# TensorE's order alone, between the input products and the stream of expert rows, redone in a one-layer hybrid encoder step

## What is computed

```python
z = rmsnorm(x) @ w_in                 # q | k | v | g | a | b, 512 columns each
o = retention(rotary(q), rotary(k), v)            # 4 heads of 128, causal with decay, state per head
y_ret  = silu(g) * groupnorm(o)
u      = a * sigmoid(b)
y_conv = silu(layernorm(depthwise_conv31(u)))
x = x + concat(y_ret, y_conv) @ w_out
h = rmsnorm(x)
qry = h @ peer_query                  # 8 heads x 2 x 128
top16 of qry . keys per half, then top16 of the 256 sums -> 16 experts of 16384 per row and head
x = x + sum_e softmax_e * gelu(h . down[e]) * up[e]
out = rmsnorm(x)
```

## Time and profile before

| | |
|---|---|
| median of 3 runs | 1663.01 us (1662.77 to 1663.81) |
| the profiled execution's own time | 1664.46 us |
| its span | 1662.7 us |
| PE busy | 1383.8 us (83%) |
| DVE busy | 1174.9 us (71%) |
| ACT busy | 573.3 us (34%) |
| POOL busy | 716.7 us (43%) |
| gather queue | 570.46 MB, 82.9% of 16 DMA engines' span |
| HBM read | 604.19 MB |

### The profile page before, as it was taken

One profiled execution on the slowest core, in us unless ns is written; L12 is line 12 of the kernel. 1 busy time (PEld: TensorE's weight loads), 2 busy tenths in 40 slices (PEclk: granted clock), 3 DMA queues, 4 the chain that ended last, 5 costly groups with the idle time before them and its releaser, 6 DMA issues.

```text
span 1662.7 us, 14018 instructions
## 1 busy us (share of the span) xinstructions
PE 1383.8 (83%) x4311; PEld 678.6 (41%) x4311; DVE 1174.9 (71%) x2555; ACT 573.3 (34%) x1785; POOL 716.7 (43%) x633
## 2 busy tenths in 40 slices
PE   7999999998898789778977897789779877777733
PEld 6744465554353335324433443344324423332311
DVE  3997758966876777677767776777777777676755
ACT  3112231632433333333333333333433333333342
POOL 0004624644444445444444444445444444444552
PEclk9999999999899999999999999999999999999955
DMA  7203227999999999999999999999999999999996
GB/s 293 102 1 100 110 77 279 371 421 422 422 420 422 421 422 420 422 421 422 420 422 421 422 421 422 421 421 421 421 422 421 421 422 420 419 420 421 414 421 256
DMA packets 87978, 608.39 MB, mean 366 GB/s; under 512 B 11104, under 2 KB 13664, under 8 KB 16224
## 3 DMA queue, kind: packets, MB, share of 16 engines
q0 software_dynamic: 78336, 570.46, 82.9%
q1 hardware_dynamic: 9568, 37.04, 5.9%
HBM read 604.19 MB, written 2.88 MB: 365 GB/s over the span
## 4 chain that ended last, share of the span: by engine, by line
DMA 44%; PE 37%; DVE 10%; issue 3%; ACT 3%; POOL 2%; DVEq 0%; SPq 0%; POOLq 0%
DMA arena<-experts,expert 44%; PE ps L1686 18%; PE ps L1549 8%; PE ps L1649 5%; DVE arena L1329 4%; PE ps L1529 4%; POOL arena L603 2%; ACT weight L907 1%; ACT late L917 1%; PE ps L1508 1%; DVE cst L1305 0%; DVE cst L1308 0%; DVE picked L1312 0%; PE ps L1620 0%; ACT gl L899 0%
## 5 line engine op out<-in xcount | busy, mean ns | idle before, releaser
L1686 PE MATMUL ps<-arena,late 128*128 128x512 f32 x2016 | 950.3, 624 | 206.0 <-ACT late L917 205.7
L603 POOL DMA_INDIRECT arena<-experts,expert x544 | 645.2, 1186 | 732.4 <-PE ps L1686 627.5
L1329 DVE CUSTOM_DVE_ANT_0 arena<-arena,hn 128x1024 f32<-128x1024 f32 x544 | 656.7, 1222 | 384.9 <-DMA arena<-experts,expert 381.8
L1686 PEld LDWEIGHTS ps<-arena,late 128*128 128x128 f32 x2016 | 387.3, 198 | 745.0 <-issue 450.7
L899 ACT ACTIVATE gl<-dots 128x2 f32<-128x2 f32 (+1 forms) x274 | 55.8, 204 | 814.3 <-DVE dots L1329 814.3
L917 ACT ACTIVATE late<-cst,weight 128x128 f32<-128x128 f32 (+1 forms) x536 | 183.5, 389 | 8.8
L907 ACT ACTIVATE weight<-gl,gate 128x1 f32<-128x1 f32 x544 | 130.7, 287 | 8.9
L1549 PE MATMUL ps<-arena,hT 128*128 128x512 f32 x256 | 112.3, 598 | 0.0
L1649 PE MATMUL ps<-hT,region_b 128*128 128x272 f32 x448 | 106.9, 392 | 0.0
L1649 PEld LDWEIGHTS ps<-hT,region_b 128*128 128x128 f32 x448 | 85.1, 190 | 27.9 <-issue 12.4
L1072 DVE SCALAR_TENSOR_TENSOR region_b<-region_b,par 128x574 f32<-128x574 f32 x120 | 92.5, 813 | 4.5
(11 more groups left out here) (174 smaller groups left out, 872.1 us busy)
## 6 DMA issues: line engine op xcount, KB each, us to landing
arena<-weights SPq DMA_DIRECT2D x6, 2048.0 KB, 11.0
region_b<-head_weights SPq DMA_DIRECT2D x8, 1152.0 KB, 9.5
arena<-experts,expert POOLq DMA_INDIRECT x544, 22.4
hT<-x_turned SPq DMA_DIRECT2D x2, 1088.0 KB, 7.2
arena<-weights SPq DMA_DIRECT2D x4, 512.0 KB, 10.7
xs<-x_prompt SPq DMA_DIRECT2D x4, 512.0 KB, 10.0
arena<-weights SPq DMA_DIRECT2D x2, 1024.0 KB, 13.9
y_prompt<-xs SPq DMA_DIRECT2D x4, 512.0 KB, 3.8
```

What stands on the lines that cost most here:

```text
L603: pool.indirect_dma_start(rows_of(n), None, experts, bass.IndirectOffsetOnAxis(ap=expert[:, vt % BUFS, k:k + 1], axis=0))\
L1329: last = v.tensor_tensor_reduce(out=rows_of(n)[:, 0:D], in0=rows_of(n)[:, 0:D], in1=hn[:, tile_of(vt)], scale=1.0, scalar=0.0, op0=ALU.mul ...
L1686: last = mm(ps[:, 2 * (vt % 2) + half, :], diag[:, n % DIAGS, :], rows_of(n)[:, D + half * SEC:D + (half + 1) * SEC], start=k == first * G ...
```

## The change

Eight lines of `plan()` are written anew. No job is added or left out (101 jobs before and after), and the programs of the other engines are the same but for the counts of `s_pe` they wait for.

```diff
-    order += rows(S_Q, 2) + rows(S_K, 1) + rows(S_Q, 3) + rows(S_V, 3) + rows(S_K, 2)
-    order += [("ln_mean", 0)] + rows(S_Q, SAMPLE) + head(0) + [("ln_mean", 1), ("ln_var", 0)] + rows(S_K, 3)
-    order += [("ln_var", 1)] + scores(0) + rows(S_G, 0) + [("ret_out", 0)] + rows(S_G, 1) + [("ret_state", 0)]
-    order += rows(S_G, 2, SAMPLE) + back(0) + head(1) + rows(S_G, 3) + mix(0, 0) + mix(0, 1) + scores(1)
-    order += [("ret_out", 1)] + turn("ffn_t", 0) + [("ret_state", 1)] + head(2) + query(0) + back(1) + scores(2)
-    order += keys(0) + mix(1, 0) + [("ret_out", 2)] + mix(1, 1) + head(3) + [("ret_state", 2)] + back(2) + scores(3)
-    order += mix(2, 0) + turn("ffn_t", 1) + out(3) + head(4) + mix(2, 1) + query(1) + back(3) + scores(4) + keys(1)
-    order += mix(3, 0) + [("ret_out", 4)] + mix(3, 1) + [("ret_state", 4)] + back(4) + mix(4, 0) + mix(4, 1)
+    order += rows(S_Q, 2) + rows(S_V, 3) + rows(S_Q, 3) + rows(S_K, 1) + [("ln_mean", 0)] + rows(S_K, 2)
+    order += rows(S_Q, SAMPLE) + head(0) + [("ln_var", 0)] + [("ln_mean", 1)] + rows(S_K, 3) + scores(0)
+    order += [("ln_var", 1)] + rows(S_G, 0) + rows(S_G, 1) + [("ret_out", 0)] + rows(S_G, 2, SAMPLE)
+    order += [("ret_state", 0)] + back(0) + rows(S_G, 3) + mix(0, 0) + mix(0, 1) + head(1) + head(2) + scores(1)
+    order += [("ret_out", 1)] + turn("ffn_t", 0) + [("ret_state", 1)] + query(0) + back(1) + keys(0) + scores(2)
+    order += mix(1, 0) + [("ret_out", 2)] + mix(1, 1) + head(3) + [("ret_state", 2)] + back(2) + scores(3) + mix(2, 0)
+    order += out(3) + head(4) + turn("ffn_t", 1) + mix(2, 1) + query(1) + back(3) + keys(1) + scores(4)
+    order += [("ret_out", 4)] + mix(3, 0) + mix(3, 1) + [("ret_state", 4)] + back(4) + mix(4, 0) + mix(4, 1)
```

## The result

Six runs of the changed kernel gave a median of 1673.64 us (1670.38 to 1674.67), six of the kernel before 1663.69 us (1662.77 to 1665.25). The ratio is 1.0056, with an interval from 1.0046 to 1.0067: slower by 0.56%, 9.3 us by the ratio and 9.95 by the medians. The profiled execution took 1674.19 us (span 1672.4), 9.7 more than the one of before.

The account below looks back on a forecast made before the run. A full DMA stream of fixed length follows the last gathers held by the opening, so their delay sets the time: 6.8 us from the order plus 2.1 from TensorE's clock on 1663.0 gives 1671.9 us, range 1667.3 to 1676.5.

Parts of the forecast that it names:

- Rival 4: No change, about 1663 us, because the DMA stream has slack behind 300 us; chance 0.05.
- rival 3: Early loss partly taken up by deeper queued gathers 11 to 14 or less crowded VectorE: +4, 1667 us; chance 0.07.
- the last sign of being wrong: The prediction would be wrong if the changed profile showed the DMA full before 290 us.
- Step 1: ln_mean.0 ahead of K2: TensorE waits 3.0 us, ScalarE's list delays squares(0), and +2.8 us at mean_off(1) reaches back(0).
- Step 2: head(1) moved behind g3 and mix(0, i): 0.9 us leaves the stretch, so mix(0, 1) ends +1.9 us late.
- Step 3: ScalarE's turned_heads(1) ahead of g3's emptying: mix_add(0, 1) begins +5.6 us late, 3.7 of it new.
- Step 4: Small gains from moving head(2) (0.6 us) and keys(0) (0.4): mix(1, 0) +4.6 late, first gather +5.7.
- Step 5: ret_out.4 ahead of mix(3, 0): TensorE waits 2.5 us for VectorE's decayed scores, so lateness becomes +6.8 us.
- Step 6: TensorE's clock falls behind the new waits before ln_mean.0 and ret_out.1, at three chances in four: 2.1 us.
- rival 2: Clock falls more often, at 277 us too, or S_G load's cover goes: another 2 to 4, about 1675; chance 0.13.
- Rival 5: Faster, 1658.5 us (-4.5), if VectorE starts earlier unhindered by ScalarE's list; test: squares(0) before 150.96; chance 0.03.

Follow-up runs that it names:

- e8: Kernel before with three products that nobody reads ahead of TensorE's 2.94 us wait before back(0): 1663.80 us, ratio 0.9997.
- e5: Changed kernel with matmuls that nobody reads filling TensorE's waits before ln_mean.0, ret_out.1 and ret_out.4: 1667.92 us, ratio 1.0024.
- e6: Changed kernel with mix(3, 0) put back ahead of ret_out.4, all else as changed: 1667.52 us, ratio 1.0018.
- e1: Kernel before with ln_mean.0 ahead of product K2, V3 and K1 swapped, ln_var.0 ahead of ln_mean.1: 1663.93 us, ratio 0.9999.
- e2: Kernel before with only head(1) and head(2) moved behind mix(0, 1): 1667.36 us, ratio 1.0024.
- e4: Changed kernel with ScalarE's squares(0) ahead of the copy of K2 and its g3 activations ahead of turned_heads(1): 1669.08 us, ratio 1.0031.
- e7: Kernel before with SAMPLE's q product filling the convolution wait, both ln_means ahead of K2, head(2) and keys(0) moved, ScalarE's list following: 1658.39 us, ratio 0.9966.
- e11: Kernel before with TensorE's order of e7 but ScalarE's list left as it was: 1664.20 us, ratio 1.0001.
- e3: Kernel before with only ret_out.4 moved ahead of mix(3, 0): 1669.22 us, ratio 1.0036.
- e10: e7 run once more, unchanged: 1659.42 us, ratio 0.9972 against the kernel before.

## Why the prediction was right, and where its parts were not

Forecast 1671.9, range 1667.3 to 1676.5; measured 1673.64. The direction and the mechanism (the moment at which the last gathers leave) hold. That the size holds too is in part luck: two terms of the sum were wrong by about 3 us each, in opposite directions.

The table counts from the first transposes of the opening (26.25 in e8, 25.50 in e5, 25.82 in the changed kernel). e8 is the order of before and e5 the changed order, neither with a low clock at these places, so that e5 less e8 is the order alone, and the changed kernel less e5 is the clock. Each column is one profiled execution; where two kernels share their order and clock, such stations agree within 0.1 (the first gather of the changed kernel and of e6: 216.97 both).

| station | e8 | e5 | changed | order | clock | order, predicted |
|---|---|---|---|---|---|---|
| mean_off(1) | 130.98 | 133.12 | 134.30 | +2.1 | +1.2 | +2.8 |
| back(0) | 167.35 | 167.41 | 168.65 | +0.1 | +1.2 | +2.8 |
| ret_out.1 | 191.46 | 194.38 | 195.62 | +2.9 | +1.2 | +5.6 |
| mix(1, 0) | 203.59 | 205.25 | 207.59 | +1.7 | +2.3 | +4.6 |
| first gather | 211.76 | 214.62 | 216.97 | +2.9 | +2.3 | +5.7 |
| mix(3, 0) / ret_out.4 | 246.70 | 250.75 | 253.03 | +4.1 | +2.3 | +6.8 |
| gather 16 | 268.60 | 272.48 | 277.95 | +3.9 | +5.5 | +6.8 |

**The fixed stream.** Gather 16 +8.6, span +9.7. In all thirteen profiled executions the span ends 1367.0 to 1369.3 us behind gather 16, while gather 16 itself lies anywhere from 287.4 to 303.8. Behind gather 15 the rest is as steady (1370.4 to 1372.6), so the runs don't say which of the two it is. Rival 4 (slack in the stream) is out. So is rival 3: the loss was not taken up by deeper queues. (What the prediction held against rival 3, a queue never over full before 264 us, was misread: the DMA share is 1.01 and 1.02 in 248 to 256 us. And the last sign of being wrong, the DMA full before 290, can't serve as one, since it is 1.02 in 276 to 280 us of the changed kernel with the gap still to come.)

**Step 1** foresaw the wait (3.0; 2.80 measured), squares(0) held by ScalarE's list (156.28), and mean_off(1) late; the claim that "the 2.8 stay and reach back(0)" failed, and it is the whole error of the order's 6.8. By the order alone 2.1 stood at mean_off(1) and 0.1 reached back(0); with K2's low clock 3.3 and 1.3. VectorE made some 2 us up on the way. Part of it is one instruction: the same 128x832 sum (L1098) took 2.02 before, in the row below from its timeline of VectorE, 1.08 in e5 and 1.02 in the changed kernel (163.73 in the timeline above). gated(0) (L1078) took 1.59 before and in e5, 0.69 in the changed kernel.

```profile
159.50 2.02 DVE L1098 TENSOR_TENSOR region_b<-region_b 128x832 f32<-128x832 f32 x1 [1.46 <-ACT region_b L758]
```

GpSimd's rotary runs beside them in both, and the change shifted VectorE's steps against it by 3 to 4 us; that this is the cause was not tested. TensorE came to back(0) later itself, so it waited 1.41 there and not 4.1 (1.40 in e5, with no low clock). The moves of ret_out.0, ret_state.0 and ln_var.1, put at nothing, are what the changed kernel has here beyond e1: back(0) is at 168.65 against 167.93, so they cost about 0.7.

**Step 2** said of the fall under g3 that "the new order has this fall too". It did not: 7.03. Against the profile of before, which has the fall, that is 1.7 us by which the end of mix(0, 1) was better than predicted.

**Step 3** held almost to the digit: g3 taken at 217.17 (predicted near 219, with mix(0, 1) ending 2.2 earlier than thought), both mix_adds packed behind gated(3), 3.7 new (3.7 predicted), and 2.94 before ret_out.1. e2 makes it alone, e4 takes it away.

**Step 4** was to give 1.0 between ret_out.1 and mix(1, 0). In the changed kernel only 0.1 is seen there, because the stretch holds the low clock behind the wait before ret_out.1 (0.78 in 220 to 224 us). e5, without it, shows 1.3 from the order (10.87 us against 12.13 in e8), and the clock takes 1.1 back. The first gather is another 1.2 late behind mix(1, 0), as predicted (1.1).

**Step 5** held: a wait of 2.54 (2.5 predicted), 2.3 more lateness (2.2 predicted).

**Step 6** left out the largest fall. (Its product is also off by a little: 0.75 x 2.7 is 2.0, not 2.1.) Of the two falls that it counted, both came, and they cost 1.2 at K2 and 1.1 behind ret_out.1: 2.3 for the 2.1. At ret_out.4 it gave only a bound ("one more at 277"), in rival 2, and no part of the 2.1. The clock fell there, and stayed low from 280 to about 287 us: from +5.6 at ret_out.4 to +8.6 at gathers 15 and 16 are 3.0 us.

**The two errors together.** By the medians, with the waits filled, the changed kernel takes 1667.92 and the one before 1663.80 (e5, e8): the order without the clock is 4.1 us, where the forecast had 6.8, and the rest of the 9.3, or 5.2, is the clock, where it had 2.1. The order was 2.7 too high, all of it step 1's delay at back(0), and the clock 3.1 too low, the fall behind ret_out.4. They offset each other, and the total is better than its parts by luck.

**Rival 5** named the mechanism that e7 then built: with ScalarE no longer held by its list, squares(0) at 147.02 and back(0) nearly without a wait. That it came to 1658.4 us where the rival said 1658.5 is chance: the rival's sum has head(1) leave (0.9) and pays 2.0 for step 5, and e7 does neither. In e4, squares(0) started at 147.97, ahead of the 150.96 that it named as its test, and the kernel was still slower than before: the test was not sufficient, since ln_mean.1 behind K2 holds VectorE next.

## What to carry to other kernels

When engines follow separate fixed lists, one list can gain only what the lists that empty its banks allow: e7's TensorE order gained nothing alone (e11) and 5.9 us with three calls of ScalarE moved. Put a job that waits for another engine behind a long product that waits for nothing, not ahead of it (step 5 and e6, 6 us). Where no such work is at hand, a few matmuls that nobody reads can keep the clock (three waits in e5, 5.7 us; one wait in e8, nothing that the median shows). And in a kernel that ends in a full stream, follow the last gathers that the opening holds back: here the end moved with them within 2.3 us. Before adding a delay up along the chain, ask at each engine whether it makes the delay up: of the 2.1 us that the order put on VectorE, 0.1 came out at back(0).

## What was unexpected of the hardware

**How long the low clock lasts.** Behind 2.54 us idle, the granted clock was 0.54 and 0.61 in two windows of 4 us running, and the products took 2.4 us longer (16.35 for 14); behind 2.94 in the earlier trace rows it was low for about half as long and cost 1.7.

**Not every wait is followed by it.** 2.80, 2.94, 2.83 and 2.54 us were; in e2 2.96 and 2.94 were not, with the same instructions behind them. Shorter waits differ too: 2.02 in e3 was followed by it, 2.03 in the earlier trace rows was not, and the wait of 0.96 before mix(4, 0) was followed by a granted clock of 0.67 and 0.50 in the two windows of 2 us from 286 us on in e10, but by 1.00 in e7, which is the same order. The product of e10, then of e7:

```profile
285.79 5.37 PE L1546 MATMUL ps<-arena,region_b 128*32 128x128 f32 x128 [0.96 <-issue]
```

```profile
285.01 3.97 PE L1546 MATMUL ps<-arena,region_b 128*32 128x128 f32 x128 [0.96 <-issue]
```

The length of the wait alone doesn't tell the two apart. This agrees with the rule of the Trainium skill (TensorE: Matmul & The Clock Gate, The HAM clock gate) that the monitor runs free.

**The opening differs from one execution to the next.** In 10 to 14 us the kernel before had 15 matmuls and the changed one 10, though the lists are the same there; the window of before, to be read against the first of the changed kernel's:

```profile
10.00:14.00 4.00, 4.00 (x15) 3.11 (x14) 2.34 (x9) 0.00 (x0) 0.00 (x0) 1.00 1.06 405
```

The column of the granted clock reads 1.00 in both, and the pace differs; why is open. The first transposes (L1538) start between 24.55 and 26.25 us in the profiled executions, and in the four that share TensorE's order up to back(0) (before, e2, e3, e8) back(0) follows 167.2 to 167.4 us behind them. So 0.9 of the 9.7 us between the two profiles stood there at 25 us and is no work of the change. Stations of two traces should be compared from the end of such an opening, not from zero.
